# Spreading the expert outputs with three bf16 products in place of one f32 product

## The chip, the core and the metric

The kernel runs on one core of a Trainium2 chip. The metric is device time in microseconds (us) of one execution. Below, PE is TensorE (PEld its weight loads), DVE is VectorE, ACT is ScalarE, POOL is GpSimd, SP is the engine whose queue issues most DMAs.

## The reference

One layer of a conditioned decoder, for 256 prompt tokens and 8 sample tokens that share all weights (264 tokens, width 1024, f32): attention with a paged cache, a short convolution, a gated spatial mix, and then the part that this change is about, a mixture of 64 SwiGLU experts of width 256, 8 of them for each token.

```python
x = x + gate_m * (merged @ w_out)
h2 = rmsnorm(x) * (1.0 + scale_f) + shift_f
gates = sigmoid_topk_gates(h2, w_router, b_router)      # 8 of 64 are not zero
a = einsum('td,edf->tef', h2, w_e_gate)
b = einsum('td,edf->tef', h2, w_e_up)
routed = einsum('tef,efd->td', silu(a) * b * gates[..., None], w_e_down)
x = x + gate_f * (routed + shared)
```

## The kernel before

Five instruction streams are written out by hand and meet at semaphores. The first half of the time goes to modulation, the projections, attention and the branches. The expert stage takes the second half and handles the 64 experts as 32 pairs, `pair(p)`. Each expert has 64 slots for tokens, so a pair fills the 128 partitions.

For a pair p, PE does this, in this order:

- `slots(p + 2)`: one bf16 product that puts each token's slot number into a PSUM bank, for the pair after next.
- `up(p)`: gate and up projection of the pair, 16 f32 products of 512 columns, two at a time side by side in the array (64 columns of weights each), into `pA`. It waits for both experts' weights (`wgt`) and the gathered tokens (`xt`). When it is done, semaphore `gu` counts up.
- `spread(p - 1, ..., range(4))`: four products of the pair before. The 128 rows of expert output, `yrow` (128 slots x 1024), are the weights of the product, 128 columns at a time, and the 0/1 matrix `gm` (128 slots x 264 tokens) is streamed; each product lands in one of four PSUM banks and holds, for 128 features, what this pair adds to all 264 tokens.
- `act_tr(p)`: two transposes of the gated activation, then `spread(p - 1, ..., range(4, 8))`.
- `down(p)`: the down projection, four f32 products into `pB`, then four into `pC`, for both experts. Then `dn1` counts up.

All matrix products but `slots` are f32, and each f32 product shows in the trace as two MATMUL and two LDWEIGHTS records on the line of the helper `mm` (L789).

DVE does `index(p + 2)` (L2319 to L2323: compares slot numbers, which writes `gm`, and finds the token numbers), `pick_experts`, `gate_column` (L2332), twelve of the sixteen 32x32-block transposes of the gathered tokens for the next pair (`tokens`, L2343), the gated product (L2377), eight additions of a bank to the sum `yacc` (`add`, L2352), the other four transposes, and the copy of `pB` to the first half of `yrow` (L2386, semaphore `y0`). ACT copies `pC` to the second half (L1770, `y1`).

POOL does nothing in this stage but `gather(p + 2)` (L761): an indirect DMA that fetches the pair's 128 token rows from HBM into `xs`.

SP refills weights in `refill`: after `gu` of pair p come the gate and up weights of two experts (2 MB each, L630), after `dn1` their down weights (1 MB each, L638), into a ring of four slots; what is issued after `gu` of pair p is used by pair p + 2. Three experts have places of their own outside the ring and are loaded where there is time (`KEPT`, `DOWN`, `AGAIN`), so three times a pair issues one expert's loads less.

After the last pair (31) come the last eight products of `spread`, which run over the four banks twice. DVE adds the earlier sum to the residual `xT` (`scaled`, L2355: three tiles before the copy L2386 and five behind it), then takes the eight products one by one (L2431, and L2435 for the samples), which frees the bank of each, and SP stores the result.

The tile names in the rows are those of the memory behind a name: `vtok` holds `yrow`, parts of `pT` hold `gm` and `yacc`, `qT` holds the transposed tokens, `oaT` the activations, `sinT` the gate columns.

Of the kernel before, what the change touches and what calls it, by code (L numbers as in the profile page):

```python
# [6 lines left out]
ALU = mybir.AluOpType  # L7
ACT = mybir.ActivationFunctionType
# [6 lines left out]
P = 128  # L15
D = 1024
# [93 lines left out]
def turn(i, n, per):  # L110

    return n if i is None else i * (4 * per) + n
# [95 lines left out]
def build(nc, A, O):  # L208

    with ExitStack() as ctx:  # L210
        def sb(name, shape, dt=F32):
            return ctx.enter_context(nc.sbuf_tensor(name, shape, dt))
# [20 lines left out]
        mask = sb("mask", [P, 3 * P])  # L233
# [37 lines left out]
        cm = sb("cm", [P, 3, E])  # L271
# [43 lines left out]
        gm = [free_p[:, 3 * D + a * NT:3 * D + (a + 1) * NT] for a in range(4)]  # L315
# [46 lines left out]
        def rest(b, at, n):  # L362
# [38 lines left out]
            "consts", "zeroed", "csig", "csilu", "ada_mm", "ada", "sq1", "var1", "rs1", "h1s", "h1", "eksq", "ekss", "tilesum", "adsum", "mix_done", "in_done", "gsig",  # L401
            "sqq", "varlat", "rslat", "cqn", "ckv", "krin", "krot",
# [4 lines left out]
            "merged", "x1", "sq2", "norm2", "var2", "rs2", "h2s", "h2x", "h2", "lsig", "xa", "h2tr", "raw", "gates", "gatesT", "gsel", "gbc",   # L407
            "silu", "act", "yout",
            "h2tok", "pmax", "pall", "flag", "posT", "pick", "gcol", "xt", "idx", "gu", "silu_s", "act_s", "dn0", "dn1", "y0", "y1",
# [281 lines left out]
        def _(pool):  # L691
# [10 lines left out]
            for t, n in ((cosT, "cosT"), (sinT, "sinT"), (mask, "mask"),  # L702
                         (bsp, "bsp"),
                         (brou, "brou"), (wrou, "w_router")):
                pool.dma_start(t[:], A[n]).then_inc(d_late, 16)
# [36 lines left out]
            pool.wait_ge(s["var2"], 1)  # L742
# [22 lines left out]

            gather(0, None)
# [11 lines left out]
        def _(pe):  # L778
# [638 lines left out]
            spread(NPAIR - 1, None, range(8))  # L1417
# [29 lines left out]
        def _(act):  # L1447
# [41 lines left out]
            act.wait_ge(s["var1"], 1)  # L1489
            nc.scalar.activation(rstd[:], rstd[:], ACT.Sqrt).then_inc(s["rs1"], 1)  # L1490
# [21 lines left out]
            act.wait_ge(s["var1"], 1)  # L1512
# [15 lines left out]
            act.wait_ge(s["varlat"], 1)  # L1528
            link(nc.scalar.activation(rstd[:], rstd[:], ACT.Sqrt))
            act.sem_inc(s["rslat"], 1)  # L1530
            ada_rows((4,))
            mixed_rows("cc", (0,))
            act.wait_ge(s["varlat"], 2)
            nc.scalar.activation(rstd[:], rstd[:], ACT.Sqrt).then_inc(s["rslat"], 1)
# [113 lines left out]
            for q in range(NS):  # L1648
# [30 lines left out]
                if q == 1:  # L1679
                    act.wait_ge(s["varlat"], 3)  # L1680
                    nc.scalar.activation(rstd[:], rstd[:], ACT.Sqrt).then_inc(s["rslat"], 1)
# [27 lines left out]
            act.wait_ge(s["var2"], 1)  # L1709
            nc.scalar.activation(rstd[:], rstd[:], ACT.Sqrt).then_inc(s["rs2"], 1)  # L1710
# [86 lines left out]
        def _(dve):  # L1797
# [53 lines left out]
            dve.sem_inc(s["var1"], 1)  # L1851
# [16 lines left out]
            dve.wait_ge(s["rs1"], 1)  # L1868
# [23 lines left out]
            dve.sem_inc(s["varlat"], 1)  # L1892
# [8 lines left out]
            dve.wait_ge(s["rslat"], 1)  # L1901
# [7 lines left out]
            dve.sem_inc(s["varlat"], 1)  # L1909
            dve.wait_ge(s["rslat"], 2)  # L1910
# [170 lines left out]
            def head_max(h):  # L2081
                dve.wait_ge(s["asc"], h + 1)
                link(V.tensor_tensor(am, pB[:, 0:3 * P], mask[:], ALU.add))
# [18 lines left out]
            for q in range(NS):  # L2102
# [41 lines left out]
                if q == 1:  # L2144
                    inv_var("vvar", CW, rstd[:])
                    dve.sem_inc(s["varlat"], 1)
                    dve.wait_ge(s["rslat"], 3)
# [62 lines left out]
            dve.sem_inc(s["var2"], 1)  # L2210
            dve.wait_ge(s["rs2"], 1)
# [214 lines left out]
            for p in range(29, NPAIR):  # L2426
                pair(p)
            for m in range(DT):
# [162 lines left out]
```

## Time and profile before

| | us |
|---|---|
| device time, three runs | 995.99, 997.11, 997.92 |
| median | 997.11 |
| span of the profiled execution, first to last instruction | 996.5 |
| PE busy in that span | 970.8 (97%) |
| DVE busy | 610.7 (61%) |
| ACT busy | 187.9 (19%) |
| POOL busy | 56.7 (6%) |

The span is that of one profiled execution; no device time is listed for that execution apart from the three runs, whose median lies 0.6 us over the span. Busy shares are averages over stages that have different limits, so they are read stage by stage below. The expert stage runs from 511 us to the end. "PEclk" is the granted clock of TensorE as a share of 2.4 GHz, and "DMA share" the mean busy share of the core's 16 DMA engines in that stretch.

### The profile page before, as it was taken

What the parts mean: (1) busy time and instruction counts of PE and PEld (TensorE: products, weight loads), DVE (VectorE), ACT (ScalarE), POOL (GpSimd) and SP (SyncE); (2) the same over time, 40 slices, a digit from 0 to 9 for tenths busy, and PEclk for the clock granted to TensorE, in tenths of its full rate; (3) what the DMA queues carried; (4) which work ended last, traced back from release to release, by engine and by line L of the source; (5) the groups of instructions that cost most, each with busy time, mean ns of one, the idle gap of its engine ahead of it and who ended that gap; (6) DMA issues with size and microseconds to landing.
All of it is one profiled execution on the core that took longest, in us unless ns stands there. A gap on an engine that the chain in (4) does not pass through costs nothing.

```text
span 996.5 us, 14013 instructions
## 1 busy us (share of the span) xinstructions
PE 970.8 (97%) x4542; PEld 547.3 (55%) x4542; DVE 610.7 (61%) x1563; ACT 187.9 (19%) x385; POOL 56.7 (6%) x81
## 2 busy tenths in 40 slices
PE   6999999999999999999989999999999999999997
PEld 2487766444547778888743444444444444444443
DVE  3603322468754011133738898898898898888875
ACT  3311231345444100002510100000000000001000
POOL 0100010100000000000210000000000000000000
PEclk9999999999999999999989999999999999999999
DMA  8994469555555583554679999999999999999991
GB/s 310 420 413 195 177 240 325 174 162 167 164 156 215 203 331 132 211 189 159 232 290 420 424 421 427 424 420 424 427 421 425 425 422 403 421 422 423 427 413 65
DMA packets 55211, 311.88 MB, mean 313 GB/s; under 512 B 8954, under 2 KB 28442, under 8 KB 33266
## 3 DMA queue, kind: packets, MB, share of 16 engines
q1 hardware_dynamic: 48834, 297.21, 75.2%
q0 software_dynamic: 6320, 13.93, 3.9%
q8 instruction: 32, 0.52, 0.2%
q14 instruction: 25, 0.20, 0.1%
HBM read 315.80 MB, written 3.95 MB: 321 GB/s over the span
## 4 chain that ended last, share of the span: by engine, by line
PE 82%; DMA 7%; SPq 5%; DVE 3%; issue 2%; ACT 0%; DVEq 0%; POOLq 0%; ACTq 0%
PE bank L789 48%; PE pA L789 21%; PE pB L789 6%; PE pC L789 5%; DMA ring<-in_w_e_gu 5%; SPq L456 3%; SPq L500 1%; SPq L495 1%; DMA xs<-h_rows,idx 1%; DMA pT<-in_poolT 1%; PE bank L1341 1%; PE pA L822 0%; PE pD L789 0%; DVE xT L2355 0%; DMA ring<-in_poolT 0%
## 5 line engine op out<-in xcount | busy, mean ns | idle before, releaser
L789 PE MATMUL pA<-ring,qT 128*64 128x512 f32 x976 | 228.5, 597 | 2.6 <-DMA ring<-in_w_e_gu 2.5
L2343 DVE STREAM_TRANSPOSE qT<-xs 32x256 f32<-32x256 f32 x480 | 209.2, 436 | 7.7
L789 PE MATMUL bank<-hT,ring 128*128 128x264 f32 (+1 forms) x832 | 189.3, 388 | 2.3 <-ACTq L1616 2.3
L789 PEld LDWEIGHTS bank<-hT,ring 128*128 128x128 f32 (+1 forms) x832 | 154.3, 189 | 35.6 <-issue 10.0
L789 PEld LDWEIGHTS pA<-ring,qT 128*64 128x64 f32 x976 | 72.1, 137 | 130.7 <-issue 126.8
L789 PE MATMUL bank<-pT,vtok 128*128 128x264 f32 x512 | 127.9, 393 | 0.3 <-DVE pT L2435 0.3
L789 PEld LDWEIGHTS bank<-pT,vtok 128*128 128x128 f32 x512 | 92.0, 190 | 39.3 <-issue 26.7
L2352 DVE TENSOR_TENSOR pT<-pT,bank 128x264 f32<-128x264 f32 x248 | 99.9, 427 | 8.8 <-PE bank L789 7.3
L789 PE MATMUL bank<-wuk,ring 128*128 128x512 f32 x192 | 86.3, 597 | 0.0
L789 PE MATMUL pB<-ring,oaT 128*64 128x512 f32 x240 | 62.0, 605 | 0.0
L789 PE MATMUL pC<-ring,oaT 128*64 128x512 f32 x240 | 60.3, 592 | 0.0
L789 PEld LDWEIGHTS bank<-wuk,ring 128*128 128x128 f32 x192 | 35.0, 190 | 41.6 <-issue 41.0
L761 POOL DMA_INDIRECT xs<-h_rows,idx x32 | 31.9, 998 | 420.0 <-DVE sinT L2332 401.8
L1764 ACT ACTIVATE oaT<-pA 128x256 f32<-128x256 f32 x32 | 12.3, 385 | 217.1 <-PE pA L789 217.1
L1770 ACT ACTIVATE vtok<-pC 128x512 f32<-128x512 f32 x32 | 19.2, 599 | 158.5 <-PE pC L789 158.5
L789 PE MATMUL bank<-pT,ring 128*128 128x264 f32 (+1 forms) x208 | 48.6, 388 | 0.0
L1938 DVE TENSOR_REDUCE xs<-ksq 128x8 f32<-128x512 f32 x48 | 32.3, 685 | 21.5 <-ACT ksq L1588 19.8
L2180 DVE TENSOR_TENSOR pT<-bank,pT 128x264 f32<-128x264 f32 x18 | 7.8, 433 | 61.4 <-PE bank L789 61.4
L789 PEld LDWEIGHTS bank<-pT,ring 128*128 128x128 f32 x208 | 39.3, 190 | 7.3 <-issue 0.4
L789 PE MATMUL bank<-wuk,pT 128*128 128x512 f32 x64 | 30.7, 630 | 7.7 <-DMA pT<-in_poolT 7.7
L789 PEld LDWEIGHTS pC<-ring,oaT 128*64 128x64 f32 x240 | 18.3, 137 | 35.4 <-issue 35.4
L789 PE MATMUL bank<-qT,ring 128*128 128x264 f32 x160 | 36.3, 387 | 0.3 <-DVE qT L2280 0.3
(344 smaller groups left out, 813.9 us busy)
## 6 DMA issues: line engine op xcount, KB each, us to landing
ring<-in_w_e_gu SPq DMA_DIRECT2D x61, 2048.0 KB, 17.3
ring<-in_w_e_dn SPq DMA_DIRECT2D x60, 1024.0 KB, 16.2
ring<-in_poolT SPq DMA_DIRECT2D x64, 208.0 KB, 2.8
ring<-in_w_ada SPq DMA_DIRECT2D x12, 1024.0 KB, 10.4
ring<-in_w_bg SPq DMA_DIRECT2D x4, 3072.0 KB, 11.5
ring<-in_w_mix SPq DMA_DIRECT2D x5, 2048.0 KB, 14.9
ring<-in_w_ada SPq DMA_DIRECT2D x4, 2048.0 KB, 13.9
ring<-in_poolR SPq DMA_DIRECT2D x56, 128.0 KB, 2.3
```

The lines of the kernel that those rows point to most:

```text
L456: return sp.value_load(ptab[0:1, bass.ds(x, 1)], min_val=0, max_val=NPOOL - 1)
L495: sp.dma_start(pgT[b][:, j], A["poolT"][bass.ds(page(i * (2 * NPG) + (b * NPG + j)), 1)] .rearrange("o p c -> (o p) c")).then_inc(wgt[b], 16)
L500: sp.dma_start(rowpg[g][x], A["poolR"][bass.ds(page(g * HALF + x), 1)] .rearrange("o r c -> (o r) c")).then_inc(d_rows, 16)
L761: nc.gpsimd.indirect_dma_start(out=xs[:, q % 2, :], out_offset=None, in_=h2rows, in_offset=bass.IndirectOffsetOnAxis(ap=idx[:, q % 2:q % 2 ...
L789: return nc.tensor.matmul(out, lhsT, rhs, start=start, stop=stop)
L1341: last = nc.tensor.transpose(t[:, f * P:(f + 1) * P], act_s[:, f * P:(f + 1) * P], ident[:])
L1764: nc.scalar.activation(silu_s, pA[:, 0:FE], ACT.Silu).then_inc(s["silu_s"], 1)
L1770: nc.scalar.activation(yrow[:, 512:], pC[:], ACT.Copy).then_inc(s["y1"], 1)
L1938: V.tensor_reduce(out=kss[:, q, j, :], in_=ksq[:, j % 2, :].rearrange("p (h d) -> p h d", h=H), op=ALU.add, axis=AX.X).then_inc(s["ksq_use ...
L2180: link(V.tensor_tensor(g[:, b, :], t[:, 0:NT], g[:, b, :], ALU.mult))
L2343: last = V.transpose(xTs[32 * j:32 * j + 32, q % 2, :, 32 * a:32 * a + 32], src[32 * a:32 * a + 32, j])
L2352: V.tensor_tensor(yacc[:, m, :], yacc[:, m, :], bk[n % 4][:, 0:NT], ALU.add).then_inc(free[n % 4], 1)
```

## The change

The product `yrow x gm` is no longer one f32 product. Each value of `yrow` is taken apart into three bf16 numbers: its upper 16 bits (`high_y`, a view of `yrow` itself with a step of two bf16 elements), the rest's upper 16 bits (`mid_y`), and what then remains, rounded to bf16 (`low_y`, written over the lower 16 bits of `yrow`). `gm`, whose values are 0 and 1, becomes bf16. PE adds the three products up in the same bank.

The two subtractions for each half of `yrow` are made by POOL, in `parts`, placed ahead of the pair's `gather` in POOL's order; for the second half of the last pair DVE makes them, ahead of the last additions. The last pair's products are ordered by part instead of by tile (`spread_last`). To find memory for the rest, `mask` and `cm` share one tile, and to find semaphores, eight of them became two (`var`, `root`), with the same waits at the same places.

```diff
-        mask = sb("mask", [P, 3 * P])
+        late = sb("mask_choice", [P, 3 * P + 3 * E])
+        mask, cm = late[:, 0:3 * P], late[:, 3 * P:3 * P + 3 * E].rearrange("p (j e) -> p j e", j=3)
...
-        gm = [free_p[:, 3 * D + a * NT:3 * D + (a + 1) * NT] for a in range(4)]
+        gm = [free_p[:, 3 * D + a * NT // 2:3 * D + (a + 1) * NT // 2].bitcast(BF16) for a in range(4)]
+        rest_y = [free_p[:, 3 * D + 2 * NT:3 * D + 2 * NT + 512], late[:, 0:512]]
+        high_y, low_y = (yrow.bitcast(BF16).rearrange("p (c two) -> p two c", two=2)[:, x] for x in (1, 0))
+        mid_y = [r.bitcast(BF16).rearrange("p (c two) -> p two c", two=2)[:, 1] for r in rest_y]
...
+            def parts(q, i, hf):
+
+                cols = slice(512 * hf, 512 * hf + 512)
+                pool.wait_ge(s[f"y{hf}"], turn(i, q + 1, 1))
+                nc.gpsimd.tensor_tensor(rest_y[hf], yrow[:, cols], high_y[:, cols], ALU.subtract).then_inc(s[f"mid{hf}"], 1)
+                pool.wait_ge(s[f"mid{hf}"], turn(i, q + 1, 1))
+                nc.gpsimd.tensor_tensor(low_y[:, cols], rest_y[hf], mid_y[hf], ALU.subtract).then_inc(s[f"low{hf}"], 1)
...
             with pool.Fori(0, 7) as i:
                 for b in range(4):
+                    for hf in range(2):
+                        parts(b, i, hf)
                     gather(3 + b, i)
-            gather(NPAIR - 1, None)
+            for q in range(NPAIR - 4, NPAIR - 1):
+                for hf in range(2):
+                    parts(q, None, hf)
+                if q + 3 < NPAIR:
+                    gather(q + 3, None)
+            parts(NPAIR - 1, None, 0)
...
             def spread(q, i, ms):
-                if ms[0] == 0:
+                hf = ms[0] // 4
+                if hf == 0:
                     emptied(USE["G", q], i)
-                    pe.wait_ge(s["y0"], turn(i, q + 1, 1))
+                pe.wait_ge(s[f"low{hf}"], turn(i, q + 1, 1))
                 for m in ms:
-                    if m == 4:
-                        pe.wait_ge(s["y1"], turn(i, q + 1, 1))
                     n = USE["C", q, m]
                     t = use(n, i)
-                    mm(t[:, 0:NT], yrow[:, m * P:(m + 1) * P], gm[q % 4], True, True).then_inc(full[n % 4], 1)
+                    c = slice(m * P, (m + 1) * P)
+                    mm(t[:, 0:NT], high_y[:, c], gm[q % 4], True, False)
+                    mm(t[:, 0:NT], mid_y[hf][:, m % 4 * P:(m % 4 + 1) * P], gm[q % 4], False, False)
+                    mm(t[:, 0:NT], low_y[:, c], gm[q % 4], False, True).then_inc(full[n % 4], 1)
+
+            def spread_last(q, hf):
...
-            spread(NPAIR - 1, None, range(8))
+            spread_last(NPAIR - 1, 0)
+            spread_last(NPAIR - 1, 1)
...
             for p in range(29, NPAIR):
                 pair(p)
+            dve.wait_ge(s["y1"], NPAIR)
+            V.tensor_tensor(rest_y[1], yrow[:, 512:], high_y[:, 512:], ALU.subtract).then_inc(s["mid1"], 1)
+            dve.wait_ge(s["mid1"], NPAIR)
+            V.tensor_tensor(low_y[:, 512:], rest_y[1], mid_y[1], ALU.subtract).then_inc(s["low1"], 1)
             for m in range(DT):
```

How instructions stand on POOL inside its loop, one pair, before (the DMA is the gather):

```order
L771 UNCONDITIONAL_BRANCH
L771 ISA
L758 REGISTER_ALU [waits idx]
L761 DMA xs<-h_rows,idx 128x1088 [waits gcol,xt]
L756 REGISTER_ALU
```

and with the change (`vtok` is `yrow`; `pT` and `mask_choice` are the two halves' `rest_y`):

```order
L773 TENSOR_TENSOR pT<-vtok 128x512 [waits y0]
L775 TENSOR_TENSOR vtok<-pT 128x512 [waits mid0]
L773 TENSOR_TENSOR mask_choice<-vtok 128x512 [waits y1]
L775 TENSOR_TENSOR vtok<-mask_choice 128x512 [waits mid1]
L759 REGISTER_ALU
L761 REGISTER_ALU [waits idx]
L764 DMA xs<-h2_rows,idx 128x1088 [waits gcol,xt]
```

Four subtractions now stand ahead of each gather, and the gather can't start before the second half of the output of the pair before is there (`y1`).

On DVE, from the last pair's sums to the first of the last additions, before:

```order
L2355 SCALAR_TENSOR_TENSOR xT<-pT,ada,xT 128x256
L2355 SCALAR_TENSOR_TENSOR xT<-pT,ada,xT 128x256 [waits vector_chain] x2
L2386 COPY vtok<-pB 128x512 [waits dn0,vector_chain]
L2355 SCALAR_TENSOR_TENSOR xT<-pT,ada,xT 128x256
L2355 SCALAR_TENSOR_TENSOR xT<-pT,ada,xT 128x256 [waits vector_chain] x4
L2431 SCALAR_TENSOR_TENSOR xT<-bank,ada,xT 128x256 [waits bank_full3,vector_chain]
L2435 TENSOR_TENSOR pT<-pT,bank 128x8
```

and with the change:

```order
L2423 COPY vtok<-pB 128x512 [waits dn0,vector_chain]
L2392 SCALAR_TENSOR_TENSOR xT<-pT,ada,xT 128x256
L2392 SCALAR_TENSOR_TENSOR xT<-pT,ada,xT 128x256 [waits vector_chain] x4
L2466 TENSOR_TENSOR mask_choice<-vtok 128x512 [waits y1,vector_chain]
L2468 TENSOR_TENSOR vtok<-mask_choice 128x512 [waits mid1]
L2472 SCALAR_TENSOR_TENSOR xT<-bank,ada,xT 128x256 [waits bank_full3]
L2476 TENSOR_TENSOR pT<-pT,bank 128x8
```

Two subtractions stand between the residual's sums and the last eight additions.

On PE, the last eight products, before:

```order
L789 MATMUL pC<-ring,oaT 64x512 x4
L789 MATMUL bank<-pT,vtok 128x264 [waits bank_free3,y0]
L789 MATMUL bank<-pT,vtok 128x264 [waits bank_free0]
L789 MATMUL bank<-pT,vtok 128x264 [waits bank_free1]
L789 MATMUL bank<-pT,vtok 128x264 [waits bank_free2]
L789 MATMUL bank<-pT,vtok 128x264 [waits bank_free3,y1]
```

and with the change, the first half of them complete and the start of the second, in which four upper parts come before the first middle part again:

```order
L807 MATMUL bank<-pT,vtok 128x264 [waits bank_free3,y0]
L807 MATMUL bank<-pT,vtok 128x264 [waits bank_free0]
L807 MATMUL bank<-pT,vtok 128x264 [waits bank_free1]
L807 MATMUL bank<-pT,vtok 128x264 [waits bank_free2]
L807 MATMUL bank<-pT 128x264 [waits mid0]
L807 MATMUL bank<-pT 128x264 x3
L807 MATMUL bank<-pT,vtok 128x264 [waits low0]
L807 MATMUL bank<-pT,vtok 128x264 x3
L807 MATMUL bank<-pT,vtok 128x264 [waits bank_free3,y1]
```

A bank is complete only with its low part, so all four banks of a half have to be free before the first of them is complete.

## Rows read from the trace of the kernel before

**Rows 1.** Windows of all engines: stretch, busy (instructions), PEclk, DMA share, GB/s.

```profile
900.00:950.00 50.00, 50.00 (x227) 21.87 (x224) 44.29 (x114) 4.49 (x10) 3.97 (x4) 1.00 1.01 424
```

**Rows 2.** Chain that ended last, in order of time: start, us, what.

```profile
703.75 7.02 PE pA L789 x32
710.77 1.98 PE bank L789 x8
712.75 0.22 PE bank L1341 x2
712.97 1.78 PE bank L789 x8
714.75 1.87 PE pB L789 x8
716.62 1.72 PE pC L789 x8
718.55 7.02 PE pA L789 x32
...
934.59 22.96 DMA ring<-in_w_e_gu
```

**Rows 3.** Timeline at 957 us: start, us, instruction, idle before and releaser.

```profile
957.69 7.09 PE L789 MATMUL pA<-ring,qT 128*64 128x512 f32 x32 [1.47 <-DMA ring<-in_w_e_gu]
```

**Rows 4.** Line L630, window 947 to 952 us: the last gate-and-up loads.

```profile
L630 SPq DMA_DIRECT2D ring<-in_w_e_gu x2: 333/333/333, 948.8 to 949.4; - x2
...
DMA to landing us min/median/max: 18.6/20.8/22.9
```

**Rows 5.** Windows as in Rows 1, around one of the pairs with one load less.

```profile
840.00:845.00 5.00, 5.00 (x24) 1.44 (x20) 4.83 (x12) 0.00 (x0) 1.00 (x1) 1.00 0.93 388
845.00:850.00 5.00, 5.00 (x26) 3.57 (x26) 4.56 (x12) 0.77 (x2) 0.00 (x0) 1.00 0.94 363
```

**Rows 6.** Groups by line and form: busy us, mean ns, idle before.

```profile
L789 PE MATMUL bank<-ksq 64*128 64x264 bf16 x32 | 9.2, 286 | 0.0
L789 PEld LDWEIGHTS bank<-ksq 64*128 64x128 bf16 x32 | 3.0, 93 | 24.6 <-issue 24.6
L2355 DVE SCALAR_TENSOR_TENSOR xT<-pT,ada,xT 128x256 f32<-128x256 f32 x8 | 3.9, 483 | 0.2
L1929 DVE TENSOR_TENSOR zp<-pT 128x1024 f32<-128x1024 f32 x1 | 1.2, 1227 | 7.2 <-ACT pT L1523 7.2
L726 POOL TENSOR_SCALAR_AFFINE_SELECT ring<-ring 128x1024 f32<-128x1024 f32 x1 | 1.1, 1105 | 31.9 <-DMA ring<-in_wspT 31.9
```

**Rows 7.** Timeline of a pair: POOL's gather and DVE's copy of pB.

```profile
706.02 0.99 POOL L761 DMA_INDIRECT xs<-h_rows,idx  x1 [13.88 <-DVE sinT L2332]
...
717.07 0.69 DVE L2386 COPY vtok<-pB 128x512 f32<-128x512 f32 x1
...
720.17 0.43 DVE L2332 TENSOR_SCALAR sinT<-ones,xs 64x1 f32<-64x1 f32 x2
```

**Rows 8.** Tile xs, 520 to 960 us: the gathers' time to landing.

```profile
DMA to landing us min/median/max: 8.1/10.3/11.0
```

**Rows 9.** Timeline of the end.

```profile
972.45 7.09 PE L789 MATMUL pA<-ring,qT 128*64 128x512 f32 x32
...
982.22 1.76 DVE L2352 TENSOR_TENSOR pT<-pT,bank 128x264 f32<-128x264 f32 x4 [0.24 <-PE bank L789]
...
985.50 0.69 DVE L2386 COPY vtok<-pB 128x512 f32<-128x512 f32 x1
986.11 2.56 DVE L2355 SCALAR_TENSOR_TENSOR xT<-pT,ada,xT 128x256 f32<-128x256 f32 x5
...
988.70 0.48 DVE L2431 SCALAR_TENSOR_TENSOR xT<-bank,ada,xT 128x256 f32<-128x256 f32 x1
```

**Rows 10.** Windows as in Rows 1, around PE's longest wait in this stage.

```profile
505.00:508.50 3.50, 0.54 (x3) 0.13 (x1) 0.56 (x2) 0.00 (x0) 0.44 (x2) 0.93 1.04 384
508.50:511.00 2.50, 2.30 (x9) 1.67 (x9) 0.42 (x2) 0.92 (x2) 0.00 (x0) 0.50 0.99 420
```

More of the change, by code:

```diff
@@ L406, in build @@
             "asc", "atr", "aout", "amx", "aexp", "anorm", "aPT", "oa", "z", "conv", "vcen", "sqv", "placed", "vn", "vntok", "sg", "wsp",
-            "merged", "x1", "sq2", "norm2", "var2", "rs2", "h2s", "h2x", "h2", "lsig", "xa", "h2tr", "raw", "gates", "gatesT", "gsel", "gbc",
+            "merged", "x1", "sq2", "norm2", "h2s", "h2x", "h2", "lsig", "xa", "h2tr", "raw", "gates", "gatesT", "gsel", "gbc",
             "silu", "act", "yout",
-            "h2tok", "pmax", "pall", "flag", "posT", "pick", "gcol", "xt", "idx", "gu", "silu_s", "act_s", "dn0", "dn1", "y0", "y1",
+            "h2tok", "pmax", "pall", "flag", "posT", "pick", "gcol", "xt", "idx", "gu", "silu_s", "act_s", "dn0", "dn1", "y0", "y1", "mid0", "mid1", "low0", "low1",
             "fgates", "turn")}
@@ L1368, in spread @@
             def spread(q, i, ms):
-                if ms[0] == 0:
+                hf = ms[0] // 4
+                if hf == 0:
                     emptied(USE["G", q], i)
-                    pe.wait_ge(s["y0"], turn(i, q + 1, 1))
+                pe.wait_ge(s[f"low{hf}"], turn(i, q + 1, 1))
                 for m in ms:
-                    if m == 4:
-                        pe.wait_ge(s["y1"], turn(i, q + 1, 1))
                     n = USE["C", q, m]
                     t = use(n, i)
-                    mm(t[:, 0:NT], yrow[:, m * P:(m + 1) * P], gm[q % 4], True, True).then_inc(full[n % 4], 1)
+                    c = slice(m * P, (m + 1) * P)
[3 more added lines that the diff above has]
+            def spread_last(q, hf):
+                ms = range(4 * hf, 4 * hf + 4)
+                if hf == 0:
+                    emptied(USE["G", q], None)
+                pe.wait_ge(s[f"y{hf}"], q + 1)
+                for m in ms:
+                    mm(use(USE["C", q, m], None)[:, 0:NT], high_y[:, m * P:(m + 1) * P], gm[q % 4], True, False)
+                pe.wait_ge(s[f"mid{hf}"], q + 1)
+                for m in ms:
+                    mm(bk[USE["C", q, m] % 4][:, 0:NT], mid_y[hf][:, m % 4 * P:(m % 4 + 1) * P], gm[q % 4], False, False)
+                pe.wait_ge(s[f"low{hf}"], q + 1)
+                for m in ms:
+                    n = USE["C", q, m]
+                    mm(bk[n % 4][:, 0:NT], low_y[:, m * P:(m + 1) * P], gm[q % 4], False, True).then_inc(full[n % 4], 1)
             def pair(p, i=None):
@@ L1488, in _ @@
             early_squares(4, 8)
-            act.wait_ge(s["var1"], 1)
-            nc.scalar.activation(rstd[:], rstd[:], ACT.Sqrt).then_inc(s["rs1"], 1)
+            act.wait_ge(s["var"], 1)
+            nc.scalar.activation(rstd[:], rstd[:], ACT.Sqrt).then_inc(s["root"], 1)
             ada_rows((1,))
@@ L1527, in _ @@
             mixed_rows("cb", range(4))
-            act.wait_ge(s["varlat"], 1)
+            act.wait_ge(s["var"], 2)
             link(nc.scalar.activation(rstd[:], rstd[:], ACT.Sqrt))
-            act.sem_inc(s["rslat"], 1)
+            act.sem_inc(s["root"], 1)
             ada_rows((4,))
             mixed_rows("cc", (0,))
-            act.wait_ge(s["varlat"], 2)
-            nc.scalar.activation(rstd[:], rstd[:], ACT.Sqrt).then_inc(s["rslat"], 1)
+            act.wait_ge(s["var"], 3)
+            nc.scalar.activation(rstd[:], rstd[:], ACT.Sqrt).then_inc(s["root"], 1)
             mixed_rows("cc", (1, 2, 3))
@@ L1679, in _ @@
                 if q == 1:
-                    act.wait_ge(s["varlat"], 3)
-                    nc.scalar.activation(rstd[:], rstd[:], ACT.Sqrt).then_inc(s["rslat"], 1)
+                    act.wait_ge(s["var"], 4)
+                    nc.scalar.activation(rstd[:], rstd[:], ACT.Sqrt).then_inc(s["root"], 1)
                 if q == 2:
@@ L1708, in _ @@
                                      scale=ada[:, 4, m, 0:1]).then_inc(s["xa"], 1)
-            act.wait_ge(s["var2"], 1)
-            nc.scalar.activation(rstd[:], rstd[:], ACT.Sqrt).then_inc(s["rs2"], 1)
+            act.wait_ge(s["var"], 5)
+            nc.scalar.activation(rstd[:], rstd[:], ACT.Sqrt).then_inc(s["root"], 1)
             act.wait_ge(s["raw"], 1)
@@ L1900, in _ @@
             dve.sem_inc(s["krot"], 1)
[L1901 removed]
+            dve.wait_ge(s["root"], 2)
             for k in range(QT):
```

31 lines of the change are left out of this document (15 added, 16 removed).

## The prediction

> **What bounds the kernel now.** I read the windows of the expert stage first. PE is busy all the time in 900 to 950 us, which looks like a kernel bound by PE. But the DMA engines stand at 1.01 of their time in the same row, at 424 GB/s [rows 1]. Two resources are full, so the question is which of them would give way.
>
> The chain gives PE's pair: 7.02 + 1.98 + 0.22 + 1.78 + 1.87 + 1.72 us, and with the slot product some 0.2 us more, from one `up` at 703.75 to the next at 718.55, 14.80 us [rows 2]. In that time a pair asks for two experts of 3.146 MB (from the shapes), 6.29 MB, and 6.29 MB / 14.80 us = 425 GB/s, to which the gathered token rows come. That is a little more than the 424 GB/s that the engines deliver. So the loads fall behind from pair to pair. What is issued after `gu` of pair p is needed at the start of `up(p + 2)`, two pairs less one `up` later: 2 x 14.80 - 7.02 = 22.6 us. The load issued at 934.59 took 22.96 us, and there PE waited 1.47 us for it [rows 2, 3]. PE's own pace and the DMAs' pace are equal to within one percent, since three pairs that load one expert less let the DMAs catch up. A look at PE's busy share alone would miss this.
>
> The last row of this kind matters most. The last gate-and-up load was issued at 949.4 us and landed after 22.9 us, at 972.3 [rows 4]. The last `up` began at 972.45 [rows 9]. So whatever PE gains before 972 us, the last `up` can't begin sooner unless that load lands sooner.
>
> **Part 1, the spread on PE.** Eight f32 products take 1.98 + 1.78 = 3.76 us a pair [rows 2], 16 records of about 0.22 us; a record streams the 264 columns twice, so one pass is 0.11 us. Twenty-four bf16 passes at 0.11 us are 2.64 us, 1.1 us less. The upper bound of a bf16 pass is the slot product, which stands alone between two other groups: it costs the chain 0.2 us (its record, 286 ns, overlaps with the next; its weight load takes 93 ns [rows 6]). I take 0.11 us, since weight loads of f32 are hidden in this same place. Not all of the 1.1 us is a gain: the second four products wait for banks that DVE's additions free, at 1.76 us for four [rows 9]. That leaves 0.5 to 1.1 us of a pair.
>
> None of it is on the path while the DMAs are full. It goes to PE's wait for weights. It is worth something only where the DMA queue had run low because PE issued too late: in 840 to 850 us the rate fell to 388 and 363 GB/s [rows 5]. What is missing there is (36 + 61) x 5 us / 424 = 1.1 us. A PE that is 0.5 us a pair or more ahead since its last wait, four pairs earlier, issues the loads after this low point 2 us or more earlier and fills it. The last load then lands 1.1 us earlier, and so does the last `up`: **-1.1 us**, between 0 and -1.5 (neighbouring windows may be a little low too).
>
> **Part 2, POOL's subtractions in the loop.** Each is 128 x 512 with two f32 inputs. No such POOL instruction is in the trace. The nearest is a select with one input, 1105 ns for 1024 elements, 0.54 us for 512 [rows 6]; two inputs and an output taken one after the other would be three times that, 1.6 us. I take 1.1 us, two inputs by one price each. The Trainium skill (GPSIMD Engine Reference, section 3.1) gives 4497 ns for 2048 elements, from which an estimate would be 1.1 us for 512; no run here shows it yet.
>
> Behind the four subtractions waits the gather, and behind it DVE's gate columns and transposes, on which the next `up` waits. Before, `y0` is there at about 717.8 - 14.8 = 703.0, the gather starts at 706.0 and lands 10.3 us later (at most 11.0), at 716.3 to 717.0, for a use at 720.17 [rows 7, 8]. Four subtractions of 1.1 us with 0.1 us between them end at 707.8, so the gather lands at 718.1 to 718.8, and 1.4 to 2.1 us are left. The pair shrinks by 0.5 us where PE is free. So the cover holds: **0 us**. The products themselves wait for `low0` and `low1` (705.4, 707.8), while they stand behind an `up` that ends at 710.8: 0 us too.
>
> **Part 3, the end.** After the last load PE runs `up` and the rest as before, and DVE is the chain from 982 us on. DVE's wait of 0.24 us for the second four banks goes [rows 9]: **-0.2 us**.
>
> DVE's five residual sums run until 988.7, and then its last eight additions begin at once [rows 9]. Now two subtractions of 128 x 512 stand between. 1227 ns for 1024 elements and 483 ns for 256 [rows 6] put one at 0.61 (half of the first) to 0.73 us (on the line between them). Twice 0.69: **+1.4 us** (1.2 to 1.5). ACT's half of `yrow` is there before, and POOL's half needs two subtractions from 986.2, until 988.6, before DVE is done: covered.
>
> The last eight products go over four banks twice. The first four additions free the banks at the pace of DVE. Before, one product in the second round could start with each bank. Now no bank is complete until the fourth is free and its upper part, four middle parts and one low part have run: 6 x 0.11 us and the latency of a product beyond its pass, 0.286 - 0.11: 0.84 us, and a semaphore: **+0.9 us** (0.5 to 1.2). In the first round there is no such wait, since DVE comes last there.
>
> The merged semaphores and the shared tile keep every wait where it was: 0 us.
>
> Sum: -1.1 - 0.2 + 1.4 + 0.9 = **+1.0 us**. The span of 996.5 becomes 997.5; the median of 997.1 lies 0.6 over that span, so the forecast is **998.1 us**.
>
> **The rivals.**
>
> *DVE and POOL block each other.* In the end stretch POOL's two subtractions (2.2 us) and DVE's five sums (2.56 us [rows 9]), which read two tiles of SBUF each, want to run at the same time, just ahead of the last additions. If one has to stand still while the other runs, DVE is late by both of POOL's instructions, +2.2 us, and the time is **1000.3 us**. In the loop DVE would wait only for the rest of one POOL instruction, in the index step, which the loads' slack absorbs. Before, no POOL instruction that reads SBUF meets a DVE instruction with two SBUF inputs, so no row speaks for or against. The Trainium skill (SBUF — State Buffer, "Who interferes with whom") states just this rule: a DVE instruction with two SBUF inputs and a POOL instruction that reads SBUF exclude each other for a whole instruction.
>
> *The gather becomes late (slower).* From a subtraction of 1.6 us on, the four end at 709.8 and the gather lands at 720.1 to 720.8, at or after its use; each 0.1 us more then costs 0.4 us over the loop of two pairs. At 2.0 us that is about 0.5 us a pair over 30 pairs, with the DMAs idle in between: 15 us, less where the loads were behind anyway. About **1010 us**. My 1.1 us speaks against it; the unknown start-up of a POOL instruction for it.
>
> *Bf16 passes don't run at 0.11 us (slower).* At 0.21 us each the eight products take 5.0 us, 1.3 us more than before, and the pair 16.1 us against the 14.9 us that it takes on average: 30 x 1.2 = 36 us, **1034 us**. The weights are read with a step of two elements, which no row shows. Against it: the f32 weight loads in this same place are hidden, since the records follow one another at 0.22 us [rows 2].
>
> *PE's clock falls (slower).* PE idled about 3 us before 508.5, and in the next window its granted clock was 0.50, the lower level of 1.2 GHz [rows 10]. After the 1.47 us wait it stayed at the upper one. Waits now grow to about 2 us. If the clock fell before the last but one `up`, the last `up` would be about 1.7 us late: **999.8 us**.
>
> *PE was the bound after all (faster).* If the DMA engines could deliver more, 30 pairs would each be 0.5 us shorter or more: 998.1 + 1.1 - 15 = **984 us**. The share of 1.01 and the wait at 957 us speak against it.
>
> **How the numbers follow.** Forecast 0.40; blocking 0.27; late gather 0.12; slow passes 0.04; clock 0.05; faster 0.12. The unknown prices spread the forecast from 996.5 (more of the low point filled, lower ends of the end terms) to 999.5, and blocking from 999 to 1002. The range of 996.0 to 1006.0 holds these, the clock's case and the mild part of the late gather. A measurement of this kernel tells 0.2%, 2.0 us, from no change: 995.1 to 999.1 counts as the same. Of the forecast 0.31 falls inside, 0.07 above, 0.02 below; of blocking 0.06 inside and 0.21 above; of the clock's case 0.02 and 0.03. So faster 0.14, same 0.39, slower 0.47.
>
> **What the profile of the changed kernel would show.** Right: DMA share 1.0 at 424 GB/s in 550 to 950 us, PE's busy time down, and waits of PE for `in_w_e_gu` in many pairs, up to 2 us each; the last `up` near 971.3; no low windows after the third pair with one load less; POOL's TENSOR_TENSOR near 1.1 us; on DVE two of 0.7 us before the last additions, and one wait of 0.9 us among these. Blocking: DVE's five sums stretched, or gaps between them, and the same on POOL. Late gather: DVE waiting for `xs` with the DMA share under 1. Wrong altogether: fewer than 2 us of added PE waits with a shorter time, or LDWEIGHTS of bf16 that PE waits for.

## The result

The change makes the kernel slower: 1008.56 us against 997.25 us for the kernel before, measured side by side, a ratio of 1.0119 with a 95% interval of 1.0101 to 1.0136. The forecast was 998.1 us, its range ended at 1006.0 us.

First the page of the changed kernel: busy time by engine, then two groups by line and form, and one of the DMA issues (size, median time to landing).

```profile
PE 950.2 (95%) x4798; PEld 521.5 (52%) x4798; DVE 635.0 (63%) x1565; ACT 187.6 (19%) x385; POOL 192.4 (19%) x207
...
L807 PE MATMUL bank<-pT,vtok 128*128 128x264 bf16 x512 | 98.0, 278 | 3.4 <-DVE pT L2476 2.7
...
L807 PEld LDWEIGHTS bank<-pT,vtok 128*128 128x128 bf16 x512 | 50.0, 98 | 45.2 <-issue 35.2
...
ring<-in_w_e_gu SPq DMA_DIRECT2D x61, 2048.0 KB, 13.4
```

PE is busy 20.6 us less than before, as was meant. DVE is busy 24.3 us more, though only two instructions were given to it. And the gate-and-up loads land after 13.4 us in the median, where the page of the kernel before has 17.3 us. A load that lands sooner had fewer others ahead of it, so the DMA queues are shorter.

What PE waited for in 530 to 975 us shows it too, before and then changed (total us, times, longest):

```profile
PE pA L789 <- DMA ring<-in_w_e_gu: 2.5, 3, 1.5
```

```profile
PE bank L1359 <- DVE pT L2389: 28.2, 28, 1.0
```

Before, PE waited for loads. Now it never does: once a pair its transposes wait for the bank that DVE's first addition frees.

The windows that answer to [rows 5] and [rows 1] show where the queues run dry (stretch, busy time and instructions of PE, PEld, DVE, ACT, POOL, then PEclk, DMA share, GB/s):

```profile
840.00:845.00 5.00, 5.00 (x25) 1.52 (x23) 3.94 (x9) 0.60 (x1) 3.14 (x3) 1.00 0.88 339
845.00:850.00 5.00, 5.00 (x28) 1.81 (x25) 4.83 (x14) 0.38 (x1) 2.17 (x3) 1.00 0.54 191
850.00:855.00 5.00, 3.98 (x29) 2.35 (x28) 4.91 (x14) 0.38 (x1) 0.00 (x0) 1.00 0.89 305
900.00:950.00 50.00, 46.93 (x248) 18.55 (x246) 44.94 (x110) 4.69 (x10) 17.39 (x17) 1.00 1.01 425
```

The low point at the pair with one load less was to be filled; instead it became deeper, from 388 and 363 GB/s to 339, 191 and 305 GB/s. Where all loads are issued the share is full again. So the pair of the changed kernel is longer than the loads need on average, but not by much.

What fills the pair is DVE. Some of its groups in 550 to 950 us, before and then changed (busy us, mean ns, idle before):

```profile
L2321 DVE SCALAR_TENSOR_TENSOR oaT<-pT,cosT 128x264 f32<-128x264 f32 x27 | 11.7, 433 | 4.3 <-DVE pT L2319 4.3
...
L2296 DVE TENSOR_SCALAR ksq<-ones,ident 64x64 bf16<-64x64 f32 x52 | 10.6, 244 | 0.0
```

```profile
L2380 DVE STREAM_TRANSPOSE qT<-xs 32x256 f32<-32x256 f32 x420 | 183.0, 436 | 6.7
L2389 DVE TENSOR_TENSOR pT<-pT,bank 128x264 f32<-128x264 f32 x208 | 75.1, 424 | 0.1
L2358 DVE SCALAR_TENSOR_TENSOR oaT<-pT,cosT 128x264 f32<-128x264 bf16 x27 | 28.6, 1060 | 4.3 <-DVE pT L2356 4.3
L2333 DVE TENSOR_SCALAR ksq<-ones,ident 64x64 bf16<-64x64 f32 x52 | 24.3, 504 | 0.0
```

Two groups of DVE take more than twice their time: the index step goes from 433 to 1060 ns, and the two picks from 244 to 504 ns in the mean (of the six in 600 to 640 us the shortest takes 237 ns and the longest 773, so one of the two is long and the other isn't). That is 0.63 + 2 x 0.26 = 1.15 us a pair. The transposes keep theirs (436 ns), and so do the additions (424 ns), which have no POOL instruction beside them. The timeline of one pair shows what stands beside them (start, us, instruction, idle before and releaser):

```profile
704.62 1.03 POOL L773 TENSOR_TENSOR pT<-vtok 128x512 f32<-128x512 f32 x1 [9.62 <-DVE vtok L2423]
...
705.35 0.49 DVE L2356 TENSOR_SCALAR pT<-bank,sinT 128x264 bf16<-128x264 f32 x1 [0.82 <-PE bank L807]
705.73 1.04 POOL L775 TENSOR_TENSOR vtok<-pT 128x512 bf16<-128x512 f32 x1
706.00 1.06 DVE L2358 SCALAR_TENSOR_TENSOR oaT<-pT,cosT 128x264 f32<-128x264 bf16 x1 [0.16 <-DVE pT L2356]
706.73 1.23 POOL L773 TENSOR_TENSOR mask_choice<-vtok 128x512 f32<-128x512 f32 x1
...
707.24 0.93 DVE L2333 TENSOR_SCALAR ksq<-ones,ident 64x64 bf16<-64x64 f32 x2
708.04 1.04 POOL L775 TENSOR_TENSOR vtok<-mask_choice 128x512 bf16<-128x512 f32 x1
708.09 0.42 DVE L2369 TENSOR_SCALAR sinT<-ones,xs 64x1 f32<-64x1 f32 x2
```

The index step begins at 706.00 beside a POOL instruction that ends at 706.77, and ends 0.29 us behind it, as if most of it had stood still until then. The picks begin beside the next one, which ends at 707.96, and end 0.21 us behind it. That POOL instruction takes 1.23 us, not 1.04. The step on L2356, which reads a PSUM bank and one column of SBUF, ran beside a POOL instruction in its usual 0.49 us, and so did the two gate columns on L2369 (0.42 us for both; 205 ns each in 550 to 950 us, 208 before).

Two stretches of time account for the whole loss. From DVE's copy of the first pair (p = 0) to that of the last it is the loop of 31 pairs; from that last copy to the final sum (L2363 before, L2400 now) it is the end. Before:

```profile
524.32 0.69 DVE L2386 COPY vtok<-pB 128x512 f32<-128x512 f32 x1 [3.08 <-PE pB L789]
...
992.63 0.22 DVE L2363 TENSOR_TENSOR cT<-pT,ada 128x64 f32<-128x64 f32 x1
```

With the change (the additions of the last eight products are left out but for the first and the fifth):

```profile
520.97 0.69 DVE L2423 COPY vtok<-pB 128x512 f32<-128x512 f32 x1 [3.08 <-PE pB L807]
...
989.24 0.69 DVE L2423 COPY vtok<-pB 128x512 f32<-128x512 f32 x1
989.85 3.88 DVE L2392 SCALAR_TENSOR_TENSOR xT<-pT,ada,xT 128x256 f32<-128x256 f32 x5
993.76 0.69 DVE L2466 TENSOR_TENSOR mask_choice<-vtok 128x512 f32<-128x512 f32 x1
994.49 0.73 DVE L2468 TENSOR_TENSOR vtok<-mask_choice 128x512 bf16<-128x512 f32 x1
995.11 0.47 DVE L2472 SCALAR_TENSOR_TENSOR xT<-bank,ada,xT 128x256 f32<-128x256 f32 x1
...
998.64 0.48 DVE L2472 SCALAR_TENSOR_TENSOR xT<-bank,ada,xT 128x256 f32<-128x256 f32 x1 [1.60 <-PE bank L807]
...
1000.72 0.23 DVE L2400 TENSOR_TENSOR cT<-pT,ada 128x64 f32<-128x64 f32 x1
```

With the last copy of before at 985.50 [rows 9] the loop takes 461.2 us before and 468.3 us now, **+7.1 us**, and the end 7.1 and 11.5 us, **+4.4 us**. The store behind it ends 0.5 us later. What came ahead of the loop was 3.4 us shorter in this execution; in two of the experiments below, which have the same code up to there (the gather first, and the last pair in f32), the first copy starts at 524.02 and 523.97, so it is not the change's. Together 8.6 us, as the spans say (996.5 and 1005.1). The medians are 11.3 us apart because the two executions lie on different sides of theirs. This one took 1006.85 us, the shortest of the four of the changed kernel. In every run on record with both values the device time is 1.7 to 1.9 us over the span, so the span of 996.5 of the kernel before stands for 998.2 us or a little more, above its median.

### The profile page after: what moved, and what is told of

It is laid out like the page before. It is cut to its first block, busy times and chain, and to the rows that moved or that the text cites. A ratio compares the mean times of both kernels' runs of the same rounds, so it can differ in the third digit from the quotient of the medians.

```text
span 1005.1 us, 14674 instructions
## 1 busy us (share of the span) xinstructions
PE 950.2 (95%) x4798; PEld 521.5 (52%) x4798; DVE 635.0 (63%) x1565; ACT 187.6 (19%) x385; POOL 192.4 (19%) x207
## 4 chain that ended last, share of the span: by engine, by line
PE 59%; DVE 23%; issue 10%; SPq 5%; DMA 2%; DVEq 1%; ACT 0%; POOLq 0%; ACTq 0%
PE bank L807 42%; DVE qT L2380 13%; PE pB L807 6%; PE pC L807 5%; SPq L459 3%; PE pA L807 2%; DVE pT L2356 1%; DVE pT L2389 1%; PE bank L1359 1%; SPq L503 1%; DVE ksq L2333 1%; DVE sinT L2369 1%; SPq L498 1%; DVE oaT L2414 1%; DMA pT<-in_poolT 1%
## 5 line engine op out<-in xcount | busy, mean ns | idle before, releaser
L807 PE MATMUL bank<-pT,vtok 128*128 128x264 bf16 x512 | 98.0, 278 | 3.4 <-DVE pT L2476 2.7
L773 POOL TENSOR_TENSOR pT<-vtok 128x512 f32<-128x512 f32 x32 | 33.2, 1037 | 305.4 <-DVE vtok L2423 305.4
L2389 DVE TENSOR_TENSOR pT<-pT,bank 128x264 f32<-128x264 f32 x248 | 89.6, 424 | 0.1
L807 PEld LDWEIGHTS bank<-pT,vtok 128*128 128x128 bf16 x512 | 50.0, 98 | 45.2 <-issue 35.2
L1359 PE MATMUL bank<-ident,oaT 128*128 128x128 f32 x64 | 14.0, 300 | 28.6 <-DVE pT L2389 28.2
L773 POOL TENSOR_TENSOR mask_choice<-vtok 128x512 f32<-128x512 f32 x31 | 37.7, 1216 | 0.0
## 6 DMA issues: line engine op xcount, KB each, us to landing
ring<-in_w_e_gu SPq DMA_DIRECT2D x61, 2048.0 KB, 13.4
```

The costliest lines, as they stand in the source:

```text
L773: nc.gpsimd.tensor_tensor(rest_y[hf], yrow[:, cols], high_y[:, cols], ALU.subtract).then_inc(s[f"mid{hf}"], 1)
L807: return nc.tensor.matmul(out, lhsT, rhs, start=start, stop=stop)
L1359: last = nc.tensor.transpose(t[:, f * P:(f + 1) * P], act_s[:, f * P:(f + 1) * P], ident[:])
L2389: V.tensor_tensor(yacc[:, m, :], yacc[:, m, :], bk[n % 4][:, 0:NT], ALU.add).then_inc(free[n % 4], 1)
```

## Experiments in the loop

Theory A: POOL's subtractions hold up DVE's index step and picks. Theory B: the index step is slow because `gm`, its input, is bf16 now.

**The gather ahead of the subtractions.** POOL starts its four instructions later, beside DVE's transposes; nothing is taken away.

```diff
                 for b in range(4):
+                    gather(3 + b, i)
                     for hf in range(2):
                         parts(b, i, hf)
-                    gather(3 + b, i)
```

(and so in the pairs behind the loop).

> POOL issues each gather ahead of the four subtractions instead of behind them, so that the subtractions run while DVE transposes (one SBUF input) and no longer beside the index step and the expert picks. Theory A (POOL's subtractions hold up DVE's index step and picks, and DVE's chain sets the pair): the index step goes from 1.06 back to 0.43 us, a pick from 0.50 to 0.24 us, the pair from 15.2 to at most 14.9 us where loads allow, DMA share back to 1.0; the end stays as long as in the changed kernel; about 1000 us. Theory B (the index step is slow because its input gm is bf16): the step stays at 1.06 us and the time at 1007 to 1009 us.

Measured: 1010.27 us, ratio 1.012 (1.0097 to 1.0144). The same two groups, and a window:

```profile
L2358 DVE SCALAR_TENSOR_TENSOR oaT<-pT,cosT 128x264 f32<-128x264 bf16 x28 | 12.1, 434 | 4.4 <-DVE pT L2356 4.4
...
L2333 DVE TENSOR_SCALAR ksq<-ones,ident 64x64 bf16<-64x64 f32 x54 | 11.1, 244 | 0.0
```

```profile
850.00:900.00 50.00, 48.83 (x265) 20.98 (x265) 44.38 (x118) 4.87 (x11) 16.45 (x16) 1.00 1.01 421
```

Both steps are back at 434 and 244 ns, with `gm` still bf16: B falls, A holds. The transposes, which now have the subtractions beside them, keep their 436 ns. From 600 to 950 us the DMA share is 1.01, and PE waits for the loads (15.6 us in 530 to 975 us), as was forecast for the changed kernel. Yet the time is no better, against the 1000 us expected, because of something new at the first pair:

```profile
528.20 1.00 POOL L764 DMA_INDIRECT xs<-h_rows,idx  x1 [13.56 <-DVE sinT L2369]
540.58 1.03 POOL L773 TENSOR_TENSOR pT<-vtok 128x512 f32<-128x512 f32 x1 [11.37 <-issue]
...
542.86 0.40 PE L807 MATMUL bank<-pT,vtok 128*128 128x264 bf16 x1 [9.94 <-POOL vtok L775]
```

`y0` had long been there. The view of line L773 has two entries of POOL's queue at 529.3, both MODIFY_POOL_CONFIG; POOL began 11.3 us after them, with no releaser, and PE stood still for 9.9 us of this time. It happened once: in the next pair the subtraction followed its gather at once.

**The subtractions behind the index step.** POOL waits for the semaphore of the index step before its first subtraction; the gather stays behind them.

```diff
                 for b in range(4):
+                    pool.wait_ge(s["idx"], turn(i, 3 + b + 1, 1))
                     for hf in range(2):
                         parts(b, i, hf)
```

> In the loop POOL waits for the index step of the pair's gather before it starts the subtractions; the gather stays behind them. Theory A: the index step is back at 0.43 us, the picks stay stretched (0.5 us or more each), the gather starts about 1 us later than in the changed kernel; the pair is 15.2 - 0.6 = 14.6 to 14.9 us; 1001 to 1003 us. Theory B: the step stays at 1.06 us; 1008 us.

Measured: 1005.59 us, ratio 1.0076 (1.0057 to 1.0096); 1001 to 1003 us were expected. The hold-up follows the place of POOL's work: the index step is free, the picks, which come next, are not.

```profile
L2334 DVE TENSOR_SCALAR ksq<-ones,ident 64x64 bf16<-64x64 f32 x54 | 27.6, 549 | 0.0
...
L2359 DVE SCALAR_TENSOR_TENSOR oaT<-pT,cosT 128x264 f32<-128x264 bf16 x28 | 12.8, 456 | 4.4 <-DVE pT L2357 4.4
```

Half of the 1.15 us a pair is gone: many pairs now take 14.88 us, where the changed kernel has 15.24, and the DMA engines are busy again (424 GB/s in 800 to 850 us). The loop takes 466.0 us. The start-up is here as well, and the expectation did not have it: PE waited 7.7 us for POOL once. This run also speaks against another reading, that the earlier gather is what the first experiment gained: here the gather starts later, 5.3 us behind the index step (719.00 and 713.69) and not 3.2 as in the changed kernel (709.23 and 706.00), and the pair is shorter all the same. In the changed kernel DVE never waited for the gathered rows.

**The f32 product with POOL's work beside it.** The kernel before, with the four subtractions of every pair but the last written to memory that nothing reads, and `spread` still waiting for them.

```diff
+            def parts(q, i, hf):
...
+                nc.gpsimd.tensor_tensor(low_r[hf], rest_y[hf], mid_y[hf], ALU.subtract).then_inc(s[f"low{hf}"], 1)
...
+                    for hf in range(2):
+                        parts(b, i, hf)
                     gather(3 + b, i)
```

> The f32 product of the kernel before with f32 gm, while POOL makes the same four subtractions a pair (all but the last pair, with one more wait between the halves), which write to memory that nobody reads; the products wait for them as in the changed kernel. Theory A: index step about 1.06 us and picks about 0.50 us as in the changed kernel, pair 15.6 to 15.9 us, the end as before: 1020 to 1028 us. Theory B: index step 0.43 us, pair 14.8 us, 997 to 999 us.

Measured: 1019.74 us, ratio 1.0219 (1.0196 to 1.0242), just under the 1020 to 1028 us expected.

```profile
L2344 DVE SCALAR_TENSOR_TENSOR oaT<-pT,cosT 128x264 f32<-128x264 f32 x25 | 26.3, 1053 | 4.0 <-DVE pT L2342 4.0
L2319 DVE TENSOR_SCALAR ksq<-ones,ident 64x64 bf16<-64x64 f32 x50 | 23.4, 506 | 0.0
```

With an f32 `gm` the index step takes 1053 ns: that settles B. The loop takes 484.2 us, 15.9 us more than with the bf16 products, and a pair 15.75 us where the changed kernel has 15.24. So the bf16 products are worth 0.5 us a pair here, about half of the 1.1 us by which they shorten PE's spread. That agrees with the order of the work: only the second half of the spread stands behind DVE's held-up instructions, while the first half runs beside them.

**The upper part alone.** One bf16 product in place of three, no subtraction at all. It leaves out the middle and low parts.

```diff
-                    mm(t[:, 0:NT], high_y[:, c], gm[q % 4], True, False)
-                    mm(t[:, 0:NT], mid_y[hf][:, m % 4 * P:(m % 4 + 1) * P], gm[q % 4], False, False)
-                    mm(t[:, 0:NT], low_y[:, c], gm[q % 4], False, True).then_inc(full[n % 4], 1)
+                    mm(t[:, 0:NT], high_y[:, m * P:(m + 1) * P], gm[q % 4], True, True).then_inc(full[n % 4], 1)
```

> Leaves out the subtractions and the middle and low products: the spread uses only the upper bf16 part of yrow, gm stays bf16. PE has some 1.8 us less a pair than in the changed kernel, POOL only gathers. Theory A: index step 0.43 us, and the loads bound the loop: the last up starts 0 to 1.5 us before that of the kernel before, the whole takes 994 to 997 us. Theory B: index step 1.06 us. The rival of the prediction (PE was the bound and the DMAs had room): 30 pairs of 1.5 us less or more, under 975 us.

Measured: 995.92 us, ratio 0.9985 (0.9973 to 0.9997).

```profile
650.00:700.00 50.00, 44.94 (x209) 14.69 (x211) 45.09 (x123) 4.79 (x11) 3.96 (x4) 1.00 1.01 423
```

PE has 5 us of 50 to spare and the DMA engines deliver 423 GB/s, no more. This takes away a further 1.8 us of PE's work a pair, and the loop is 0.5 us shorter in all than that of the kernel before, 460.6 us. The loads bound this loop, and a spread of a third of the products buys 0.15% (0.03 to 0.27%).

## Experiments at the start and the end

**The last pair in f32.** The changed kernel, but for the last pair's products, which are f32 again, with an f32 `gm` of their own and without their subtractions.

```diff
-            parts(NPAIR - 1, None, 0)
...
-                for m in ms:
-                    mm(use(USE["C", q, m], None)[:, 0:NT], high_y[:, m * P:(m + 1) * P], gm[q % 4], True, False)
...
+                for m in range(4 * hf, 4 * hf + 4):
...
+                    mm(t[:, 0:NT], yrow[:, m * P:(m + 1) * P], gm_last, True, True).then_inc(full[n % 4], 1)
...
-            dve.wait_ge(s["y1"], NPAIR)
-            V.tensor_tensor(rest_y[1], yrow[:, 512:], high_y[:, 512:], ALU.subtract).then_inc(s["mid1"], 1)
-            dve.wait_ge(s["mid1"], NPAIR)
-            V.tensor_tensor(low_y[:, 512:], rest_y[1], mid_y[1], ALU.subtract).then_inc(s["low1"], 1)
```

> The changed kernel with one edit: the last pair's spread is the f32 product again, and the four subtractions of that pair are gone. Theory A (the change costs time in two separate places: 7.4 us over the loop, where GpSimd's subtractions hold up VectorE's index step and picks, and 3.8 us between the last up step and the last instruction of VectorE: 1.3 us in the five weighted sums, 1.4 us for VectorE's two subtractions, the rest the second round of banks at the halved clock): only the second place goes, so 1008.6 - 3.8 = 1004.8 us (1003.5 to 1006), the index step stays at 1.06 us and the five sums take 2.56 us again. Theory C (the end only shows what the loop left over, as a slower clock there, and the subtractions themselves cost nothing): under 1 us less, 1007.6 us or more.

Measured: 1005.26 us, ratio 1.0084 (1.0068 to 1.0101), 3.3 us less than the changed kernel. The end:

```profile
992.17 0.69 DVE L2418 COPY vtok<-pB 128x512 f32<-128x512 f32 x1
992.78 2.56 DVE L2387 SCALAR_TENSOR_TENSOR xT<-pT,ada,xT 128x256 f32<-128x256 f32 x5
999.30 0.23 DVE L2395 TENSOR_TENSOR cT<-pT,ada 128x64 f32<-128x64 f32 x1
```

The five sums take 2.56 us again and the end 7.1 us, while the loop keeps its 468.2 us. The two losses are separate, and theory C falls. (A and C are numbered anew in this expectation; its A is the account with two places.)

**GpSimd used early.** The kernel with the gather first, and one small subtraction ahead of the loop.

```diff
+        early = sb("early", [P, 8])
...
             gather(2, None)
+            nc.gpsimd.tensor_tensor(early[:], ones[:, 0:8], ones[:, 0:8], ALU.subtract)
             with pool.Fori(0, 7) as i:
```

> The kernel with the gather ahead of the four subtractions, and one edit more: after the third gather, before the loop, GpSimd does one subtraction of 128x8 into a tile of its own. In the kernel without it the first two-input instruction on GpSimd started 11.4 us after it could, while TensorE stood still for 9.9 us. Theory D (a start-up that belongs to GpSimd's first two-input instruction after its all-reduce, done once): it moves ahead of the loop, where GpSimd has nothing to do, the first real subtraction starts within 1 us of y0, and the time is 1010.3 - 9.9 = 1000.4 us (999 to 1002), which is before plus the end's 3 to 4 us, since the loop is bound by the loads again. Theory E (the 11 us belong to the loop's entry or to the gather that stands ahead, not to the first use): the wait stays, 1009 to 1011 us.

Measured: 1003.35 us, ratio 1.0065 (1.0045 to 1.0085).

```profile
521.44 0.20 POOL L783 TENSOR_TENSOR early<-ones 128x8 f32<-128x8 f32 x1 [7.11 <-issue]
528.48 1.25 POOL L765 DMA_INDIRECT xs<-h_rows,idx  x1 [6.84 <-DVE sinT L2371]
529.76 1.05 POOL L774 TENSOR_TENSOR pT<-vtok 128x512 f32<-128x512 f32 x1
```

Now the small instruction waits 7.1 us (the two queue entries stand at 514.4), and the first real one begins 0.03 us after its gather: the start-up belongs to the first instruction of this kind in the kernel and is paid once, as D says. Whether the all-reduce ahead of it matters was not tested. The loop takes 461.3 us, that of before (461.2), so all of the 7.1 us of the loop are accounted for by the hold-up. The median is above the 999 to 1002 us expected, for two reasons. The start-up had not cost its whole 9.9 us: the loop with it took 468.5 us, 7.2 more than without. And I had the end at 3 to 4 us; it is 4.3 us here, and the store adds 0.5.

**Both.** The gather first, GpSimd used early, the last pair in f32.

> The kernel before this one, and the last pair's spread in f32 again with none of its subtractions. If the three costs found are all there are (the hold-up in the index step and picks, the start-up, the end), it should be the kernel before, but for a spread that TensorE does faster behind full DMAs: 996.5 us (995 to 998), within 0.2% of before, DMA share 1.0 through the loop. If the bf16 products or the subtractions cost something further in the loop, it stays above 999 us. If TensorE had been the bound all along it would be near 985 us.

Measured: 997.88 us, ratio 0.9999 (0.9986 to 1.0013).

| kernel | loop | end | device time, median |
|---|---|---|---|
| before | 461.2 | 7.1 | 997.25, 997.27, 997.5 |
| changed | 468.3 | 11.5 | 1008.56 |
| last pair f32 | 468.2 | 7.1 | 1005.26 |
| gather first, used early | 461.3 | 11.5 | 1003.35 |
| both | 462.2 | 7.1 | 997.88 |

(Loop and end from one profiled execution each, by the two stretches above.) In the medians the end's repair is worth 3.3 us in one pair of kernels and 5.5 us in the other, the loop's 5.2 and 7.4 us. The traces give 4.4 and 7.1 us; each ratio is known to some 2 us, so they agree no better than that. Both repairs together lead back to the kernel before, and not below it: the loads still bound the loop.

## Why the prediction was wrong

**What bounds the kernel** was right for the kernel before: the loads. It was shown by the upper part alone (PE with 5 us of 50 to spare, 423 GB/s) and by the combined kernel (997.88 us). That PE was the bound, the faster rival, is refuted. It was wrong for the changed kernel: the forecast put PE's gain into waits for weights, and there were none.

**Part 1, PE's pace**, was right. The 24 products show at steps of 0.11 to 0.12 us, with weight loads of 98 ns hidden behind them, and the last two pairs, where DVE has nothing left to index, follow one another at 13.80 us, before at 14.77: 1.0 us less where 1.1 was worked out. Slow passes, a rival, did not come. The **-1.1 us** for the low point at 840 to 850 us did not come either. With the loop free again, in the combined kernel, the point is filled in part (366 and 420 GB/s where before had 388 and 363):

```profile
840.00:845.00 5.00, 5.00 (x32) 2.35 (x29) 4.82 (x13) 0.69 (x2) 3.26 (x4) 1.00 0.93 366
845.00:850.00 5.00, 5.00 (x30) 2.03 (x29) 4.08 (x11) 0.28 (x2) 0.00 (x0) 1.00 1.00 420
```

and the last `up` began at 973.46 and not before 972.45 [rows 9]. Another rival stands behind that, the one of the clock, which did not come in the loop of the changed kernel but comes here, in the `up` before the last:

```profile
957.92 8.78 PE L809 MATMUL pA<-ring,qT 128*64 128x512 f32 x32 [2.08 <-DMA ring<-in_w_e_gu]
```

It takes 8.78 us where most others take 7.09. The granted clock was 0.54 in its first 3 us, after a wait of 2.08 us (0.83 us of work in the 2.9 us ahead of it), and the last `up` follows without a wait: 1.7 us, the price that this rival named. Only with the upper part alone was the low point filled (411 and 433 GB/s), for 0.5 us of the loop. That PE ran ahead far enough to fill it was argued and not read from a row.

**Part 2, POOL in the loop**, holds the step that failed: its **0 us** for the subtractions beside DVE, where the loop became 7.1 us longer. The price of a subtraction, 1.1 us, was right (1.03 to 1.04 us when undisturbed). The estimate from the Trainium skill, GPSIMD Engine Reference, section 3.1, was as near. The gather was in time, as worked out: DVE never waited for `xs`, and the late gather, a rival, did not come. But I asked only who waits for POOL's queue, not what POOL's instructions do to those beside them. The rival that asked this put it at the end alone and said of the loop that DVE "would wait only for the rest of one POOL instruction, in the index step, which the loads' slack absorbs". Both halves of that sentence were wrong. DVE stands still for two: once in the index step (0.63 us) and once in the picks (0.52 us). And DVE has no slack of that size. Its work from the index step to the gated product and the first addition, then PE's transposes, second half of the spread, `down` and `slots`, then the next index step, form a ring. In the timeline of the changed kernel it takes 15.23 us (one `up` starts at 705.25, the next at 720.48), where the loads need 14.9 on average (461.2 us for 31 pairs); without the 1.15 us it would take 14.1, and the kernel with the gather first shows pairs of 14.17 us. The 0.8 us in between were the slack, and 1.15 us is more by 0.35 us. Over the loop it cost 0.23 us a pair (7.1 / 31), since not every pair is of this kind. The chain of before ran through PE and the loads alone [rows 2], and I took this for room on DVE, without working out DVE's own ring.

**Part 3, the end**, had two of the three terms and too low a sum: +2.3 us forecast for the stretch behind the last copy (the -0.2 us, which lies ahead of it, came), +4.4 us measured. The two subtractions took 1.42 us, as said (1.4). The second round's wait was 1.60 us in place of 0.9, because PE had stood idle for 2.7 us just ahead and its granted clock fell:

```profile
990.00:995.00 5.00, 2.53 (x16) 0.93 (x12) 4.79 (x7) 0.60 (x1) 2.31 (x2) 1.00 0.01 2
995.00:1000.00 5.00, 3.34 (x12) 1.50 (x12) 3.40 (x15) 0.00 (x0) 0.00 (x0) 0.54 0.34 109
```

```profile
995.80 1.71 PE L807 MATMUL bank<-pT,vtok 128*128 128x264 bf16 x4 [2.71 <-DVE pT L2476]
997.30 1.09 PE L807 MATMUL bank<-pT,mask_choice 128*128 128x264 bf16 x4
```

At 0.54 of the clock, mostly the lower level of 1.2 GHz, a product takes some 0.22 us of its group (the next group starts at 998.18, 0.88 us behind this one of four) and not 0.11. The prediction had the row that shows such a fall after an idle time [rows 10] and applied it only to the loop. The rest is the blocking rival's: the five sums took 3.88 us and not 2.56, **+1.3 us** where it said 2.2. They share this time with two POOL subtractions (990.02 to 992.40), and the loop's timeline suggests why it is less: DVE waits for the rest of a running POOL instruction, not for the whole of both.

**The rival that came true** was the blocking of DVE and POOL, with its mechanism right and its place mostly wrong. DVE's index step and residual sums, which read two tiles of SBUF, wait until POOL's running instruction has ended; the transposes, with one tile of SBUF, and the step that reads PSUM don't. The Trainium skill (SBUF — State Buffer, "Who interferes with whom") says the same, and the trace agrees with 433 and 1060 ns for the same step. The first pick waits too, though it reads one tile and one column, while the gate columns, which also read one tile and one column, don't; why is not shown. The late gather's 1010 us lies near the measured 1008.56 by chance: no gather was late.

## What to carry over

Before giving work to an idle engine, list what will run beside it and which of these pairs exclude each other, then work out the ring of the engine that is held up, with its own slack; an engine that is not in the chain may be less than a microsecond from it. A gain on an engine behind full DMA queues was worth next to nothing here, but a loss counts as soon as it is larger than the slack. And moving an instruction's place can undo a loss: here one gather moved ahead of four subtractions gave all of the loop's loss back, once GpSimd's start-up was paid ahead of the loop. Without that it gave nothing (1010.27 us).

## What was not expected of the hardware

- The first two-input instruction of GpSimd began 7.1 to 11.4 us after it could (11.37 us after a gather, 7.11 and 7.48 us for one of 128x8 ahead of the loop). Two MODIFY_POOL_CONFIG entries of POOL's queue stand at the head of these waits (529.3, 514.4 and 513.3 us). In the changed kernel they stand at 512.5, and the first subtraction begins at 521.75, as soon as `y0` is there: the wait of 9.33 us for `y0` covers the start-up. What passes in the time behind the entries, and why it is longer in one kernel than in another, is not shown.
- Of DVE's instructions with one tile and one scalar column, both in SBUF, the first pick (64x64) is held up (to 773 ns in the changed kernel, 244 ns without POOL beside it), and the gate columns (64x1) beside a running POOL instruction are not. The same form with its data from PSUM is not either (0.49 us).
- POOL is held up as well, by less: of its four subtractions in a pair the third took 1.23 us, and the others 1.03 to 1.04.
- A wait of PE for weights can cost more than its length. In the combined kernel the `up` behind the waits of 2.02 and 2.08 us took 8.78 us in place of 7.09, and in the kernel with the gather first and GpSimd used early so did those behind 1.96 and 1.79 us, but not that behind 2.12 us.
